# Other start addresses for the matmul operands in a fp32 decoder trunk on one Trainium2 core

## The reference, cut to what matters

```python
def swiglu_ffn(h, w_gu, w_down):
    g, u = jnp.split(h @ w_gu, 2, axis=-1)
    return (jax.nn.silu(g) * u) @ w_down
...
def reference(...):
    for i in range(DEPTH):
        x = x + 0.5 * swiglu_ffn(rmsnorm(x, n_ffn1[i]), ffn1_w_gu[i], ffn1_w_down[i])
        h = rmsnorm(x, n_mix[i])
        ...
        x = x + mix
        x = x + mem_cross_attn(rmsnorm(x, n_xattn[i]), rmsnorm(mem, n_mem[i]),
                               x_w_q[i], x_w_kv[i], x_w_o[i])
        x = x + 0.5 * swiglu_ffn(rmsnorm(x, n_ffn2[i]), ffn2_w_gu[i], ffn2_w_down[i])
    return rmsnorm(x, n_final)
```

## Time and profile before

| | |
|---|---|
| Runs, median | 2128.45 us |
| Profiled execution: span from the first to the last instruction | 2124.5 us |
| The median of the runs less that span | 3.95 us |
| TensorE matmul (PE) busy | 2079.2 us, 98% |
| Weight loads (PEld), beside it | 1737.9 us, 82% |
| VectorE (DVE) busy | 951.8 us, 45% |
| ScalarE (ACT) busy | 707.9 us, 33% |
| GpSimd (POOL) busy | 143.8 us, 7% |
| Mean granted TensorE clock | 0.983 of 2.4 GHz |
| Moved by DMA | 197.10 MB, mean 93 GB/s |

### The profile page before, as it was taken

How to read it: one execution, slowest core, us unless ns; L and a number is a source line. 1 busy time by engine, 2 the same in 40 slices (tenths; PEclk the granted TensorE clock), 3 DMA queues, 4 the chain that set the end, 5 groups by cost and what they waited for, 6 DMA issues and landing times.

```text
span 2124.5 us, 24589 instructions
## 1 busy us (share of the span) xinstructions
PE 2079.2 (98%) x9938; PEld 1737.9 (82%) x9938; DVE 951.8 (45%) x997; ACT 707.9 (33%) x833; POOL 143.8 (7%) x120
## 2 busy tenths in 40 slices
PE   7999999999999999999999999999978999999998
PEld 6888888789998888888888888888877888888886
DVE  5343333476455454433433443443287444433333
ACT  4222222354354443222222422232135433222212
POOL 3000001000001001000000000000063010000000
PEclk9999999998899999999999999999989999999999
DMA  4222223211123323333222332222333123222221
GB/s 159 91 89 98 94 95 106 84 60 60 60 84 116 100 80 119 99 99 99 87 97 94 99 98 92 88 92 89 99 114 107 52 80 99 99 99 97 88 97 54
DMA packets 192652, 197.10 MB, mean 93 GB/s; under 512 B 3506, under 2 KB 191024, under 8 KB 192592
## 3 DMA queue, kind: packets, MB, share of 16 engines
q1 hardware_dynamic: 191632, 194.00, 28.0%
q0 software_dynamic: 928, 2.25, 0.3%
q10 hardware_dynamic: 32, 0.01, 0.0%
HBM read 194.15 MB, written 2.10 MB: 92 GB/s over the span
## 4 chain that ended last, share of the span: by engine, by line
PE 90%; DVE 5%; ACT 2%; issue 1%; DMA 0%; POOLq 0%; POOL 0%; DVEq 0%; ACTq 0%
PE ps L294 30%; PE ps L296 29%; PE ps L295 29%; DVE w_lo L1280 2%; ACT w_hi L904 1%; DVE sums L1658 0%; PE ps L677 0%; DMA raw<-in_x_w_kv 0%; DVE sums L1678 0%; DVE up L1820 0%; PE ps L736 0%; DVE h_lo L1283 0%; DVE b L1394 0%; ACT p_tok L1089 0%; ACT h_hi L904 0%
## 5 line engine op out<-in xcount | busy, mean ns | idle before, releaser
L294 PE MATMUL ps<-h_hi,w_hi 128*128 128x512 f32 (+1 forms) x1728 | 672.8, 389 | 8.8 <-DVE x L1708 4.0
L295 PE MATMUL ps<-h_lo,w_hi 128*128 128x512 f32 (+1 forms) x1728 | 669.2, 387 | 0.0
L296 PE MATMUL ps<-h_hi,w_lo 128*128 128x512 f32 (+1 forms) x1728 | 669.0, 387 | 0.0
L1280 DVE TENSOR_TENSOR w_lo<-raw,w_hi 128x2048 fp32r<-128x2048 f32 (+2 forms) x189 | 420.3, 2224 | 484.9 <-ACT w_hi L904 484.9
L904 ACT ACTIVATE w_hi<-raw 128x2048 fp32r<-128x2048 f32 (+2 forms) x189 | 346.4, 1833 | 279.9 <-PE ps L296 279.9
L294 PEld LDWEIGHTS ps<-h_hi,w_hi 128*128 128x128 f32 x1728 | 326.9, 189 | 75.9 <-issue 9.4
L295 PEld LDWEIGHTS ps<-h_lo,w_hi 128*128 128x128 f32 x1728 | 326.9, 189 | 65.9 <-issue 1.0
L296 PEld LDWEIGHTS ps<-h_hi,w_lo 128*128 128x128 f32 x1728 | 326.7, 189 | 66.0
L294 PE MATMUL ps<-mid_hi,w_hi 128*128 128x512 f32 x704 | 278.4, 395 | 0.0
L296 PE MATMUL ps<-mid_hi,w_lo 128*128 128x512 f32 x704 | 278.2, 395 | 0.0
L295 PE MATMUL ps<-mid_lo,w_hi 128*128 128x512 f32 x704 | 278.2, 395 | 0.0
(11 more groups left out here) (284 smaller groups left out, 1965.6 us busy)
## 6 DMA issues: line engine op xcount, KB each, us to landing
raw<-in_ffn_w_gu SPq DMA_DIRECT2D x88, 1024.0 KB, 5.0
raw<-in_ffn_w_down SPq DMA_DIRECT2D x32, 1024.0 KB, 4.9
raw<-in_x_w_kv SPq DMA_DIRECT2D x16, 1024.0 KB, 5.3
raw<-in_ffn_w_down SPq DMA_DIRECT2D x16, 768.0 KB, 4.2
raw<-in_gla_w_in SPq DMA_DIRECT2D x12, 1024.0 KB, 5.1
raw<-in_x_w_q SPq DMA_DIRECT2D x8, 1024.0 KB, 5.0
raw<-in_x_w_o SPq DMA_DIRECT2D x8, 1024.0 KB, 5.0
raw<-in_gla_w_out SPq DMA_DIRECT2D x8, 512.0 KB, 3.4
```

The lines of the kernel that those rows point to most:

```text
L294: nc.tensor.matmul(out_ap, left[0], right[0], start=first, stop=False)
L295: nc.tensor.matmul(out_ap, left[0], right[1], start=False, stop=False)
L296: return nc.tensor.matmul(out_ap, left[1], right[0], start=False, stop=last)
L1280: return nc.vector.tensor_tensor(out_ap, value, hi.bitcast(F32), ALU.subtract)
```

## The change

The two weight buffers are declared flat with 64 bytes to spare. Slot 0 starts 16 bytes past a multiple of 64, slot 1 starts 48 past one (12 elements, after the 8192 bytes of slot 0). A small unused tensor `phase` of 32 bytes moves the shared area so that each region starts at a multiple of 64. Within it, `mid_hi` and `mid_lo` start 8 bytes past a multiple of 64 and `xo_hi` and `xo_lo` 12 bytes past one. Four regions behind `mid` move 128 bytes up to keep clear of it. The other regions and `h` are at 0. The instructions of each engine, their order, shapes and waits stay the same; only addresses differ.

New positions, as in the list above: `w` held at 16 or 48 (even and odd pieces) with `h`, `o`, `p`, `m` streamed from 0, `mid` from 8, `xo` from 12; `w` streamed from 16 or 48 with `h` or `m` held at 0; `xq` and `xk`, `xv` and `pT` both at 0.

```diff
-        w_hi, w_lo = sb("w_hi", [P, 2, C, COLS], F32R), sb("w_lo", [P, 2, C, COLS], F32R)
+        w_hi_flat, w_lo_flat = sb("w_hi", [P, 2 * C * COLS + 16], F32R), sb("w_lo", [P, 2 * C * COLS + 16], F32R)
+
+        def slots(flat):
+            n = C * COLS
+            return [flat[:, first:first + n].rearrange("p (k n) -> p k n", k=C) for first in (4, n + 12)]
+
+        w_hi, w_lo = slots(w_hi_flat), slots(w_lo_flat)
...
+        sb("phase", [P, 8])
+
...
+        def region_at(name, offset, shape, by):
+            flat = region(name, offset, [P, shape[1] * shape[2] + 8], F32R)
+            return flat[:, by:by + shape[1] * shape[2]].rearrange("p (c s) -> p c s", c=shape[1])
+
         x_tok = region("x_tok", 0, [P, T, D])
-        vec_rows = region("vec_rows", 88 * KB, [P, P])
-        first_rows = region("first_rows", 89 * KB, [P, P])
-        mid_hi = region("mid_hi", 0, [P, FC, SEQ], F32R)
-        mid_lo = region("mid_lo", 44 * KB, [P, FC, SEQ], F32R)
+        vec_rows = region("vec_rows", 88 * KB + 128, [P, P])
+        first_rows = region("first_rows", 89 * KB + 128, [P, P])
+        mid_hi = region_at("mid_hi", 0, [P, FC, SEQ], 2)
+        mid_lo = region_at("mid_lo", 44 * KB + 64, [P, FC, SEQ], 2)
...
-        mem_tok = (region("mem_tok0", 20 * KB, [P, MT, D]), region("mem_tok1", 88 * KB, [P, MT, D]))
+        mem_tok = (region("mem_tok0", 20 * KB, [P, MT, D]), region("mem_tok1", 88 * KB + 128, [P, MT, D]))
...
-        xo_hi, xo_lo = region("xo_hi", 56 * KB, [P, C, SEQ], F32R), region("xo_lo", 80 * KB, [P, C, SEQ], F32R)
+        xo_hi, xo_lo = region_at("xo_hi", 56 * KB, [P, C, SEQ], 3), region_at("xo_lo", 80 * KB, [P, C, SEQ], 3)
...
-                return w_hi[:, s, kk, cs], w_lo[:, s, kk, cs]
+                return w_hi[s][:, kk, cs], w_lo[s][:, kk, cs]
...
-                                              (w_hi[:, w % 2, kk, :], w_lo[:, w % 2, kk, :]), kk == 0, kk == C - 1)
+                                              (w_hi[w % 2][:, kk, :], w_lo[w % 2][:, kk, :]), kk == 0, kk == C - 1)
...
-                hi_part(w_hi[:, s, 0:nrows, :], raw[:, s, 0:nrows, :]).then_inc(sig.w_hi_ready, 1)
+                hi_part(w_hi[s][:, 0:nrows, :], raw[:, s, 0:nrows, :]).then_inc(sig.w_hi_ready, 1)
...
-                lo_part(w_lo[:, s, 0:nrows, :], raw[:, s, 0:nrows, :], w_hi[:, s, 0:nrows, :])\
+                lo_part(w_lo[s][:, 0:nrows, :], raw[:, s, 0:nrows, :], w_hi[s][:, 0:nrows, :])\
```

## The result

The changed kernel takes 2151.53 us (median of 2 runs, 2151.44 to 2151.62) against 2128.45 us before: ratio 1.0105, 95% interval 1.0086 to 1.0124. The forecast was 2075 us, range 2035 to 2150. The change costs 23.1 us where a gain of 53 was expected; the interval leaves out 1, so a loss is shown.

The account below looks back on a forecast made before the run. The prediction took PE's matmul pitch as the bound. Gains of 22.5 and 30.6 us, 53.1 off the 2124.5 us span, gave 2071.4; adding 3.95 gave about 2075 us, range 2035 to 2150.

Parts of the forecast that it names:

- What bounds the kernel: Whole kernel: PE is busy 98% of the span, so only a change of the matmuls' pitch can change much.
- What seems to count is the distance between the two start addresses.: 512-column matmuls: pitch follows moving start less held start, 226.6 ns at distance 0, 233.3 at 32.
- the second term: 2736 matmuls streaming `mid`, `xo`, `o` or `p`: 11.2 ns less each, 30.6 us gained; 18.3 us by merely reaching 226.6 ns.
- I take the new, uneven distances to leave about two thirds of 13.4 ns: Both kinds of 512-column matmuls: extra over column time becomes 8.9 ns, a pitch of 222.1 ns.
- The first term: 4992 matmuls streaming `h` under held weights: 4.5 ns less each, 22.5 us gained.
- The bounds: 512-column pitch between 213.2 and 236 ns: `h` gains 66.9 or loses 46.9 us, the others gain 55.0 or lose 7.4.
- The collision of two streams of reads: PE: moving operand's and next stationary operand's reads collide, making the extra of 13.4 or 20.1 ns by their relative position.
- The 256-column matmuls, VectorE, ScalarE: 1152 matmuls with 256 columns, 3.9 us either way, and engine accesses 8 to 16 bytes off: nothing taken for either.
- Rival 1: Extra follows distance smoothly, lowest at 0, highest at 32; all 512-column pitches 230.0 ns, 2136 us; chance 0.15.
- Rival 2: Positions do not matter; the step between `h` and `mid` comes from something else, 2128 us; chance 0.13.
- Rival 3: Starts not a multiple of 32 cost reads more: `mid`, `xo` 240.0 ns, `h` 233.3, 50.2 us lost, 2179 us; chance 0.13.
- The rule that PE never waits on anyone: Skill's two independent PE read ports, moving operand and weight load: pitch would not depend on either address.

Follow-up runs that it names:

- regions_moved_224: Kernel before plus an unused 224-byte tensor ahead of the regions, putting them where `h` and `w` lie modulo 256: 2109.45 us, ratio 0.9913 of before.
- the first sweep: Kernel before with flat, padded buffers, `h` and `mid` at 0, weight slots 4 to 32 bytes past a multiple of 64 across the FFNs: 2157.39 us.
- Held_narrow: Kernel before with gate and up matmuls holding 64 weight columns in FFN 1 and 32 in FFN 2 instead of 128: 2137.59 us.
- changed_lo_moved_64: Changed kernel with 64 more bytes behind each weight buffer, putting `w_lo` at `w_hi`'s position modulo 128: 2138.60 us, 1.0048 of before.

## Why the prediction was wrong, point by point

- **What bounds the kernel.** Right. PE's pitch moved; splits and counts did not, and pitch times count gives +22 to +23 us beside the measured +23.1.
- **"What seems to count is the distance between the two start addresses."** Half right. `mid` over weights behaves like `h` over weights as soon as it lies like `h`, and 226.7 against 233.3 ns was made by the 32 bytes: regions_moved_224 takes them away and gains 19.3 us, about the 18.3 that I named in the sum as the safer part of the second term. But I took the distance modulo 64, from a list in which everything was 0 or 32, and did not see that equality held modulo 8192 there. The change breaks it at a scale that modulo 64 hides: its spare bytes put `w_lo` 64 from `w_hi`, and `mid_lo` 64 from `mid_hi` modulo 256.
- **The step that failed: "I take the new, uneven distances to leave about two thirds of 13.4 ns".** The forecast wanted an extra of 8.9 ns over 213.2 in both kinds. It went up from 13.4 to 19.1 ns with `h` (232.3) and came down only from 20.1 to 18.3 ns with `mid` (231.5). The first term is +28.5 us (27.5 by the slot means) instead of -22.5, the second about -5 us instead of -30.6. I had drawn it from the rows with 256 columns, where distance 32 has the lower pitch. That does not carry over to 512 columns: in 17 combinations of positions nothing came below the 226.7 ns of equal starts. The bounds (213.2 to 236 ns for a kind) held both new pitches; the value inside them was taken on the wrong side. The upper bound was no bound for other positions: the first sweep has a slot at 237.3 ns.
- **The collision of two streams of reads.** Not borne out as I told it. Held_narrow excludes an extra that grows with the length of the load. What the 13.4 ns at equal starts are, why fewer held columns raise them, why 256 is the period, and why the same positions can have two pitches, all this stays open.
- **The 256-column matmuls, VectorE, ScalarE.** Nothing was taken, and nothing large came: the splits last as long as before, and the sum comes within some 1 us of the runs without them. PE's wait for `w_lo` in the projections that stream weights grew by 1.5 us (15.6 to 17.1).
- **The rivals.** Rival 1 (2136 us) had the sign for `h` but a lowest-at-0, smooth law; the table is not smooth, 4 bytes cost as much as 128. Rival 2 (positions do not matter) falls. Rival 3 (2179 us) was right that leaving the equal state costs `h` up to 6.7 ns, 233.3 in the even slot. It was wrong that 8 and 12 bytes make `mid` and `xo` worse, and the odd slot loses only 4.5 ns. Over the 7728 matmuls the loss is 3.0 ns on average (23.3 us), so the 5.5 ns from which it would have been over 2% were not reached. The share of matmuls that leave the equal state, put at 62% there, is 65% of the 7728 (4992).
- **What a measurement can tell.** The forecast says that a change under 2% is about what cannot be told from none. Here 1.05% was told with two runs to a side, and 0.9% in regions_moved_224.
- **The rule that PE never waits on anyone** (the Trainium skill, "SBUF — State Buffer", section Who interferes with whom) is no guide to the pitch here: with the same instructions, it moves from 226.7 to 232.3 ns with the addresses alone. The same page says of start alignment (section Operand start alignment) that it is about legality, not speed; the runs of this case time it.

## What to carry to other kernels

When a kernel is a dense stream of float32r matmuls, each with its own weight load, work out the start of every held and moving operand modulo 256 and make them all equal, high and low parts and double-buffer slots too. Two places were tried for the common start, this kernel's and 32 bytes past it (226.7 and 226.9 ns); 16 bytes past it was worse (230.0). Padding between two buffers breaks that silently, and any small tensor declared in between does. Check by the pitch from first and last start, per slot and per tensor. In most pieces it repeats to 0.1 ns, so one profile decides what many timed runs would not; but leave out the first pieces of a stage, which can have another pitch at the same positions. And where the trace shows a quantity at two settings only, do not choose a value beyond both of them because another shape hints at it; a one-line variant that merely makes the settings equal was the safe gain.

## What was unexpected of the hardware

Two operands whose starts differ by 4 bytes already cost 5.7 ns per matmul of 512 columns, and 128 bytes cost the same 5.7 ns, at the granted clock of 2.4 GHz. Two slots of one buffer, worked in turn, keep pitches of their own. Pieces with the same positions can still differ: 233.3 and then 226.7 ns in the even slot of changed_lo_moved_64. Holding a quarter of the weight columns makes a matmul's pitch 4.8 ns longer (231.5 against 226.7 ns).
